# Expert gate and up weights laid out as one block each, with 4 KB runs, in a mixture-of-experts decoder step

## The reference, cut to what matters

```
gates = einsum('tk,tke->te', wts, one_hot(eidx, 64))      # top 8 of 64, weights sum to 2.5
hg = einsum('td,edf->tef', t, w_eg)                       # gate, (64, 1024, 256)
hu = einsum('td,edf->tef', t, w_eu)                       # up,   (64, 1024, 256)
a = silu(hg) * hu * gates[:, :, None]
routed = einsum('tef,efd->td', a, w_ed)                   # down, (64, 256, 1024)
shared = dot(silu(dot(t, w_sg)) * dot(t, w_su), w_sd)
x = x + g2 * (routed + shared);  y = rmsnorm(x, norm_f)
```

## Time and profile before

| | us |
|---|---|
| median of 3 runs | 1246.63 |
| lowest, highest run | 1244.76, 1246.88 |
| the profiled execution: span from first to last instruction | 1243.9 |
| its TensorE busy | 1150.2 (92%) |
| its TensorE weight loads busy | 588.9 (47%) |
| its VectorE, ScalarE, GpSimd busy | 396.0, 245.0, 218.6 |
| its DMA: bytes, mean rate | 305.82 MB, 246 GB/s |

### The profile page before, as it was taken

The page is one execution under the profiler, slowest core; times in us unless marked ns, Lnnn a source line. Parts: engine busy times, 40 slices in busy tenths (PEclk is TensorE's granted clock), DMA queues, the critical chain, the costliest instruction groups (busy, mean ns, idle before and its releaser), DMA issues. The chain is left out here.

```text
span 1243.9 us, 14302 instructions
## 1 busy us (share of the span) xinstructions
PE 1150.2 (92%) x4176; PEld 588.9 (47%) x4176; DVE 396.0 (32%) x1070; ACT 245.0 (20%) x505; POOL 218.6 (18%) x175
## 2 busy tenths in 40 slices
PE   3799998999988999999999999999999999999960
PEld 0477454444544444544544544544544544444430
DVE  3533345424355222222222222222222222222226
ACT  1400101101101212212212212212212212122114
POOL 0000700000000122222222222222222221222214
PEclk9699998589989999999999999999999999999985
DMA  9963004330466899999999999999999999999613
GB/s 295 404 212 91 3 1 156 133 131 34 172 196 212 287 308 320 329 328 311 312 309 293 304 311 290 307 300 322 319 341 302 315 310 301 310 305 312 191 20 137
DMA packets 200623, 305.82 MB, mean 246 GB/s; under 512 B 18507, under 2 KB 165019, under 8 KB 191621
## 3 DMA queue, kind: packets, MB, share of 16 engines
q1 hardware_dynamic: 180694, 271.31, 65.0%
q0 software_dynamic: 19904, 34.18, 10.9%
HBM read 300.41 MB, written 43.50 MB: 276 GB/s over the span
## 5 line engine op out<-in xcount | busy, mean ns | idle before, releaser
L933 PE MATMUL bank<-arena 128*128 128x512 f32 x1152 | 521.0, 594 | 1.4 <-ACT arena L1233 1.4
L933 PEld LDWEIGHTS bank<-arena 128*128 128x128 f32 x1152 | 213.7, 191 | 245.4 <-issue 243.3
L955 PE MATMUL bank<-arena 128*128 128x512 f32 x576 | 262.2, 598 | 4.2 <-ACT arena L1216 4.2
L622 POOL DMA_INDIRECT moe_sums<-arena x68 | 107.5, 1582 | 514.8 <-issue 440.4
L955 PEld LDWEIGHTS bank<-arena 128*128 128x128 f32 x576 | 104.5, 191 | 110.8 <-issue 107.3
L1576 DVE COPY arena<-bank 128x512 f32<-128x512 f32 x72 | 49.9, 693 | 208.5 <-PE bank L955 208.5
L1561 DVE TENSOR_TENSOR arena<-arena,bank 128x256 f32<-128x256 f32 x72 | 30.4, 422 | 257.8 <-ACT arena L1210 257.7
L708 PEld LDWEIGHTS bank<-arena 128*128 128x128 f32 x632 | 84.5, 193 | 46.5 <-issue 34.7
L610 POOL DMA_INDIRECT arena<-h_rows,arena x70 | 71.8, 1026 | 180.9 <-DVE arena L1651 180.1
L708 PE MATMUL bank<-arena 128*128 128x128 f32 x632 | 86.8, 282 | 7.0 <-DVE arena L1333 6.2
L1640 DVE TENSOR_TENSOR arena<-arena 128x640 bf16 (+1 forms) x71 | 59.3, 835 | 70.5 <-issue 70.5
(11 more groups left out here) (214 smaller groups left out, 661.9 us busy)
## 6 DMA issues: line engine op xcount, KB each, us to landing
arena<-in_w_exp_gate SPq DMA_DIRECT2D x136, 512.0 KB
arena<-in_w_exp_up SPq DMA_DIRECT2D x136, 512.0 KB
arena<-in_w_exp_down SPq DMA_DIRECT2D x68, 1024.0 KB, 10.4
arena<-in_w_ada SPq DMA_DIRECT2D x12, 2048.0 KB, 11.1
arena<-in_w_in SPq DMA_DIRECT2D x2, 4096.0 KB, 23.2
arena<-in_w_out SPq DMA_DIRECT2D x1, 4096.0 KB, 19.8
arena<-in_x_prompt SPq DMA_DIRECT2D x4, 512.0 KB, 12.8
h_rows<-arena SPq DMA_DIRECT2D x4, 512.0 KB, 8.5
```

Source lines behind the costliest of these rows:

```text
L622: pool.indirect_dma_start(out=sums, out_offset=bass.IndirectOffsetOnAxis(ap=sidx[:, par:par + 1], axis=0), in_=Y[:, (par + NT) % 2, :], in ...
L933: ins = mm(bank[gb][0:R, :], xT[k], wts[:, k, :], start=(k == 0), stop=(k == KD - 1))
L955: ins = mm(bank[2 + f][0:R, :], aT[:, par, k, 0:R], wts[:, k, f * 512:(f + 1) * 512], start=(k == 0), stop=(k == 1))
```

## The change

The gate and up buffers keep their places and sizes and are cut otherwise: 2 by 8 by 256 numbers on a partition instead of 8 by 512, so all of gate comes first and all of up behind it. The transfers go to these blocks: the four k of a half and matrix are now one run of 4 KB on a partition in SBUF as in HBM (for the shared expert, all eight k, 8 KB). The matmul of line 933 reads for each k 256 numbers of gate and 256 of up, which are 8 KB apart, as one moving operand of 2 by 256 columns; its output in PSUM is what it was. The 8-row tile's four matmuls are written out with the new indices, with as many columns as before. The number of transfers, matmuls and waits stays.

```
-        gu_w = [view(a, (KD, 512)) for a in (W, W + 4096, hT_at, mod_at)]
+        gu_w = [view(a, (2, KD, EF)) for a in (W, W + 4096, hT_at, mod_at)]
-        sh_gu = view(W + 12288, (KD, 512))
+        sh_gu = view(W + 12288, (2, KD, EF))
...
-                sp.dma_start(sh_gu[:, :, i * EF:(i + 1) * EF],
+                sp.dma_start(sh_gu[:, i],
                              I[name][0].rearrange("(p k) f -> p k f", k=KD)).then_inc(s_shw, 16)
...
-                    sp.dma_start(gu_w[q][:, k, i * EF:(i + 1) * EF].unsqueeze(1),
+                    sp.dma_start(gu_w[q][:, i, k].unsqueeze(1),
                                  eg[i][:, ds(e, 1), k]).then_inc(s_guw[q][half], 16)
...
                     if R == NS:
-                        ins = sample_product(gb, xT[k], wts, P, k, KD - 1)
+                        for j in range(4):
+                            ins = mm(bank[gb][32 * j:32 * j + NS, 0:P], xT[k], wts[:, j // 2, k, j % 2 * P:(j % 2 + 1) * P],
+                                     start=(k == 0), stop=(k == KD - 1), tile_position=(0, 32 * j))
                         continue
-                    ins = mm(bank[gb][0:R, :], xT[k], wts[:, k, :], start=(k == 0), stop=(k == KD - 1))
+                    ins = mm(bank[gb][0:R, :], xT[k], wts[:, :, k, :], start=(k == 0), stop=(k == KD - 1))
```

## The result

| | before | after |
|---|---|---|
| median of the runs, us | 1246.59 | 1256.32 |
| lowest, highest run | 1244.76, 1246.88 | 1253.06, 1258.22 |
| the profiled execution's span | 1243.9 | 1256.3 |

The ratio is 1.0081, with a 95% interval of 1.0064 to 1.0098: 9.7 us slower. The prediction was 1245.2 us with a range of 1241 to 1256. It was wrong, and the time is nearly that of its rival "the scatters come late" (1258).

A forecast was written before the change was run, and what follows sets the result against it. TensorE was taken to set the pace at 11.65 us an item, with weights in time. The median of 1246.6 us less 1.5 us of waiting for scatters, all other terms 0, gave 1245.1, rounded up to 1245.2; range 1241 to 1256.

The forecast's parts named there:

- the scatters come late: Rival, loop: longer neighbouring packets push scatters over 10.7 us and TensorE's row selection waits; 1258 at +0.8 us; chance 0.17.
- What bounds the kernel: Main loop: TensorE sets the pace at 11.65 us an item, weights come with room, the scatter chain lies just below.
- Packets, DMA share, SyncE's wait: Profile signs: some 94,000 packets, DMA share lower by 0.03 to 0.06, SyncE's wait for TensorE longer than 126.5 us.
- The operand at 0: Expert matmuls reading two runs of 256 numbers: no cost taken, +6 us kept as a rival with chance 0.08.
- the scatters' term: Scatters beside 4 KB packets: -0.2 us each, range -0.4 to +0.8; TensorE's waiting falls from 2.0 to 0.5 us, -1.5 us.
- the 4 us named as a sign of being wrong: Loop: the prediction is wrong if TensorE's waits there add up to more than 4 us.
- the nearest row for a scatter: First gather beside 8 KB down-load packets: 8.8 us against a median of 8.0, so longer packets cost it 0.8 us.
- The price of a late scatter: Loop at +0.8 us a scatter: +11 us, 8 between 900 and 1150 us and 3 between 500 and 900 us.
- The threshold: Loop's scatter chain: some 10.7 us is the longest that a scatter may take for nothing.
- that coupling: Loop: VectorE may not choose later rows before a scatter has landed, and TensorE's row selection waits for that choice.
- The one by packet number: Rival, DMA engines: scatters take 19.6 us, each of 68 items 8.9 us longer, 1852 us; chance 0.03.
- The fast start: Rival, start of the items: first gather lands earlier, TensorE keeps its clock, -3.7 us, 1241.4 us; chance 0.14.

The follow-up runs named there:

- e1: Changed kernel with its block layout and two-run operand, but the k order interleaved so that transfers keep 1 KB runs: 1245.3 us, ratio 1.0001 to the kernel before.
- e4: Changed kernel with SyncE holding the first down loads and what follows until the first gather has landed: 1253.3 us, ratio 1.0087 to the kernel before.
- e10: Changed kernel, 4 KB runs, rows chosen before keep_rows, down loads behind next gate and up, first down load held for first gather: 1239.9 us, ratio 0.9955.
- e11: Layout with 2 KB runs, rows chosen before keep_rows, down loads behind next gate and up, first down load held for first gather: 1240.9 us, ratio 0.9960.
- e3: Changed kernel with VectorE's choice of rows for item w + 3 moved ahead of keep_rows(w): 1241.6 us, ratio 0.9977 to the kernel before.
- e7: Kernel before, 1 KB runs, with VectorE's choice of rows moved ahead of keep_rows(w): 1242.2 us, ratio 0.9982 to the kernel before.
- e8: Changed kernel with SyncE loading down weights of item w - 1 after gate and up of item w: 1243.3 us, ratio 0.9986 to the kernel before.
- e2: Changed kernel with gate and up in turns of two k, so that transfers have 2 KB runs: 1246.7 us, ratio 1.0012 to the kernel before.

## Why the prediction was wrong

*What bounds the kernel: right.* TensorE sets the pace, weights come with room to spare, and the scatter's chain was the place to watch. *Packets, DMA share, SyncE's wait: right* (94,383 against some 94,000; -0.06; 577.0 us). *The operand at 0: right.* Eight matmuls of line 935 are 3.44 us in the chain of after too:

```profile
1186.12 3.44 PE bank L935 x8
```

e1 puts the operand's cost at 0, and at 0.12% at most. The Trainium skill, "Advanced Engine Details and Errata", section "Memory Cachelines", says of PSUM that a pattern that isn't contiguous slows matmuls significantly. The two runs of 1 KB here are in SBUF, and for them these runs show no slowing; PSUM is written as before, so what the section says of it isn't tested here.

*The step that failed is the scatters' term,* "So I take -0.2 us for 4 KB ones, nearer to the byte end". It measured +0.8 us (9.6 to 10.4), the end of the range that was kept for it, and the 2.0 us of waiting, of which 0.5 were to be left, became 7.1. That is over the 4 us named as a sign of being wrong. Two readings led there.

The first gather was taken as the nearest row for a scatter, but its 8.8 us were compared with the median of gathers that had company themselves (8.0). Without the down loads beside it that gather takes 4.2 us or less (e4, e10 and e11), so 8 KB packets cost it some 4.6 us and not 0.8. That the 0.8 is also the number that a scatter then lost is chance. And the forecast let the free time that the scatters gain and the longer packets nearly cancel, though the trace had nothing on how a scatter's landing answers to free time. After shows it: the DMA share fell from 0.93 to 0.87 in 700 to 800 us and the landing rose from 9.2 to 9.7.

*The price of a late scatter: the mechanism right, the number partly by luck.* For +0.8 us the sum had +11 us, of which 8.8 came in the loop and 9.7 in the medians. But it had 8 us of them between 900 and 1150 us and 3 between 500 and 900 us. There the excess over 11.65 us for each item grew by 1.7 and by 5.8 us, since from 1000 us on the scatters hardly came later (+0.1 and 0).

*The threshold was right in kind and some 0.3 us too high.* The scatter of 10.73 us about 1100 us was read as one that costs nothing. In order of time there is idle time before the choice that waited for it:

```profile
1106.64 0.28 PE L1021 MATMUL bank<-arena 128*128 128x6 bf16 x5 [0.19 <-DVE arena L1642]
```

The 0.28 us stood in the earlier trace rows already, against 0.10 in the earlier trace rows. From the choice before to this one it is 12.02 us instead of 11.65, so that scatter was some 0.4 us too late, and the longest landing for nothing is 10.3 to 10.4 us (an estimate: 10.73 - 0.37; the stop shown above gives about as much). That is where the windows from 1000 us on already stood, and before paid 4.4 us for it, not 2.0. Read so, late scatters would have deserved more than their 0.17. e3 and e7 show that this wait is all: without the coupling the same late scatters cost nothing. The prediction named that coupling but treated it as given.

*The two rivals on the DMA queues.* The one by packet number (1852 us) is out: 8 KB runs add 1.1 us, not a multiple of the company's 4.0. It was drawn from the rule of the Trainium skill, "DMA: Bandwidth & Descriptors", section "Queues, rings and completion order", by which an engine drains some 9 to 17 descriptors of a queue before it turns to the next. From 2 to 4 KB runs the landing goes the way that the prediction drew from it (later, by 0.8 us in two pairs of runs), and not by the size that it drew; whether the rule itself holds no run here can tell. *The fast start* (-3.7 us) didn't come; e4 moved the first gather by another edit, and alone it couldn't be told in the time.

*What stays open:* why 2 KB runs cost nothing and 4 KB ones 0.8 us. No run has sizes between them, or scatters with rows of another length, or 2 KB runs with the loads as late as before. By e8 a scatter gains 1.9 us for 1.6 MB less ahead of it; by that (an estimate) the 0.64 MB more ahead of it in e2 than before should have cost 0.8 us, and they cost nothing. So 1 and 2 KB runs need not be alike. Nor is it settled how much of e8's gain is the smaller load ahead of the scatter and how much the free time behind it.

## What to carry to other kernels

Longer runs in weight loads are no gain by themselves where the loads have room: look for the small, latency-bound transfer that shares the engines with them, and compare its landing with the slack of who waits for it. Where a step waits for such a landing and others stand behind it in its queue, move them ahead of it (one line here, worth 0.2% before and 1.0% after), or space out the loads that are issued just ahead of it; here either one took all the stops away with 4 KB runs. Before a row is taken for what company costs, ask what the same transfer takes without company. And look whether the slack is really there: an item that takes 12.02 us where its neighbours take 11.65 has none left.

## What the runs showed of the hardware

- A scatter of up to 128 rows beside weight loads lands after 9.6 us with 1 KB and 2 KB runs, 10.4 to 10.5 with 4 KB and 10.7 with 8 KB ones, at one order of the loads; behind the last loads it is 6.0. The first gather lands after 8.8 to 9.7 us beside the down loads and 4.2 without them (e10, e11).
- SyncE's issue of a 512 KB transfer in the loop took 0.38 us with 4 KB and 0.42 us with 2 KB runs (medians from 430 to 1165 us; 1.05 and 1.55 at most), and 1.2 us with 1 KB runs, 7.18 at most, where it stands back to back with others. Its wait for TensorE went from 126.5 us to 561 (e2) and 577 (after).
- A stop of TensorE for a choice that comes late costs 0.25 us beyond the idle time that the profile gives for it, at full clock: in the chain of waits 0.28 against 0.10 us for the five small matmuls behind it, 0.41 against 0.34 for the next two.
